# A norm shared by three engines, with a reordered start of the first mixer, in a four-block transformer kernel

## What is computed

```python
def rms_norm_2(x, g):
    xf = x.astype(jnp.float32)
    y = xf * lax.rsqrt(jnp.mean(xf * xf, axis=-1, keepdims=True) + NORM_EPS)
    return (y * g.astype(jnp.float32)).astype(x.dtype)

def ada_modulation(c, w, b):
    mod = jax.nn.silu(c) @ w + b
    shift, scale, gate = jnp.split(mod, 3, axis=-1)
...
        shift, scale, gate = ada_modulation(c, mw, mb)
        h = rms_norm_2(x, g) * (1.0 + scale) + shift
        x = x + gate * mixer(h, *mixer_params[layer])
```

## Time and profile before

| | us |
|---|---|
| median of three runs | 2342.48 |
| lowest, highest | 2342.39, 2344.87 |
| the profiled execution | 2344.19 |
| its span | 2342.4 |
| busy: TensorE, VectorE, GpSimd, ScalarE | 1880.9, 1307.9, 735.1, 607.1 |

### The profile page before, as it was taken

How to read it: one execution, slowest core, us unless ns; L and a number is a source line. 1 busy time by engine, 2 the same in 40 slices (tenths; PEclk the granted TensorE clock), 3 DMA queues, 4 the chain that set the end, 5 groups by cost and what they waited for, 6 DMA issues and landing times. The chain is left out here.

```text
span 2342.4 us, 20225 instructions
## 1 busy us (share of the span) xinstructions
PE 1880.9 (80%) x6462; PEld 998.1 (43%) x6462; DVE 1307.9 (56%) x3171; ACT 607.1 (26%) x1370; POOL 735.1 (31%) x695
## 2 busy tenths in 40 slices
PE   6987898959877898776868777988798886877877
PEld 4555332329645444332323336756444432323332
DVE  4454300027276656667676646545756667676663
ACT  3442111114622212221221214543222222222221
POOL 0000154410103343443544420330344344444441
PEclk9998899979988999998989897998899998998989
DMA  8843899958448999999999966543999999999995
GB/s 296 316 178 145 321 401 400 401 191 242 180 160 301 409 410 410 421 422 421 421 422 415 422 289 237 187 151 107 342 409 410 412 421 422 421 421 420 410 419 239
DMA packets 211846, 786.03 MB, mean 336 GB/s; under 512 B 29243, under 2 KB 89403, under 8 KB 145948
## 3 DMA queue, kind: packets, MB, share of 16 engines
q0 software_dynamic: 85408, 547.20, 56.9%
q1 hardware_dynamic: 126332, 237.53, 28.0%
HBM read 806.56 MB, written 13.98 MB: 350 GB/s over the span
## 5 line engine op out<-in xcount | busy, mean ns | idle before, releaser
L1802 PE MATMUL psum<-peer_rows,peer_diag 128*128 128x512 f32 x2048 | 980.0, 638 | 276.1 <-ACT peer_diag L1854 275.9
L1970 DVE CUSTOM_DVE_ANT_0 peer_rows<-peer_rows,peer_norm_h 128x1024 f32<-128x1024 f32 x512 | 620.1, 1225 | 445.2 <-DMA peer_rows<-in_peer_uv,peer_expert 444.9
L1891 POOL DMA_INDIRECT peer_rows<-in_peer_uv,peer_expert x512 | 582.6, 1138 | 880.9 <-PE psum L1802 667.4
L1802 PEld LDWEIGHTS psum<-peer_rows,peer_diag 128*128 128x128 f32 x2048 | 412.0, 205 | 828.2 <-issue 500.7
L1854 ACT ACTIVATE peer_diag<-ident,peer_weight 128x128 f32<-128x128 f32 x512 | 163.5, 390 | 727.6 <-DVE peer_weight L1980 727.6
L1197 PE MATMUL psum<-moe_ring,moe_W 128*64 128x512 f32 x640 | 145.4, 600 | 17.7 <-issue 12.7
L1781 PE MATMUL psum<-peer_norm_hT,peer_q_raw 128*128 128x256 f32 x512 | 123.7, 400 | 11.3 <-DMA peer_q_raw<-in_peer_q 8.1
L1781 PEld LDWEIGHTS psum<-peer_norm_hT,peer_q_raw 128*128 128x128 f32 x512 | 101.9, 201 | 37.1 <-DMA peer_q_raw<-in_peer_q 13.1
L1270 POOL COPY moe_W<-moe_X 128x512 f32 x40 | 24.3, 614 | 269.2 <-DVE moe_piece_i L1409 206.8
L1197 PEld LDWEIGHTS psum<-moe_ring,moe_W 128*64 128x64 f32 x640 | 46.7, 138 | 113.2 <-issue 113.0
L1848 ACT ACTIVATE peer_dots<-peer_dots 128x4 f32<-128x4 f32 x128 | 26.3, 206 | 262.6 <-DVE peer_dots L1970 259.4
(11 more groups left out here) (414 smaller groups left out, 2237.0 us busy)
## 6 DMA issues: line engine op xcount, KB each, us to landing
moe_ring<-in_moe_w SPq DMA_DIRECT2D x192, 512.0 KB, 10.1
mix_mod_w<-in_mod_w SPq DMA_DIRECT2D x32, 768.0 KB, 7.5
peer_q_raw<-in_peer_q SPq DMA_DIRECT2D x32, 512.0 KB
fox_w_raw<-in_fox_in SPq DMA_DIRECT2D x32, 512.0 KB
mix_w_raw<-in_w_in SPq DMA_DIRECT2D x24, 512.0 KB
lru_mod_w<-in_mod_w SPq DMA_DIRECT2D x16, 768.0 KB
fox_mod_w<-in_mod_w SPq DMA_DIRECT2D x16, 768.0 KB, 6.2
lru_in_raw<-in_lru_in SPq DMA_DIRECT2D x22, 512.0 KB, 4.7
```

The costliest lines, as they stand in the source:

```text
L1802: ins = pe.matmul(Y(t, c), diag[:, j % 2, k, :], R[:, place_of(m), D + c * BANK:D + (c + 1) * BANK], start=first and k == 0, stop=final an ...
L1891: pool.indirect_dma_start(R[:, place_of(m), :], None, uv, bass.IndirectOffsetOnAxis(ap=expert[:, t, at:at + 1], axis=0))\
L1970: dve.tensor_tensor_reduce(here, here, norm.h[:, t, :], 1.0, 0.0, ALU.mult, ALU.add, dots[:, t, at:at + 1]).then_inc(dotted, 1)
```

## The change

Four things change. (1) In the non-plain norms VectorE scales tiles 0 and 2 and ScalarE tiles 1 and 3, each into its own part of `h`, which has been turned by then; GpSimd rounds all four; VectorE subtracts. The buffers `v` stay allocated for the mixer's squares. (2) The first weights' rounding stands behind ScalarE's tile 1 and their subtraction behind VectorE's second low half: one piece in mix1 and lru, four in fox. (3) In mix1 SP loads the c column second and modulation pieces 0 to 3 among weight pieces 0 to 7; ScalarE computes the SiLU between the squares and the root, and reloads the root's table; TensorE takes modulation pieces 0 and 1 before the first weight piece, and piece n behind weight piece n. (4) In mix1 VectorE subtracts weight piece 1 before it copies the bias curve. The norms of moe and the peers keep their work.

```diff
-    def act(self, act):
+    def v_of(self, n):
+
+        t, g = n % 2, n // 2
+        return self.h[:, t, g * BANK:(g + 1) * BANK].rearrange("p (k n) -> p k n", k=4)
+
+    def affine(self, act, n, out):
+        act.wait_ge(self.turned, n + 1)
+        for k in range(4):
+            f, src = 4 * (n // 2) + k, self.bank(n % 2, n // 2)[:, k, :]
+            if self.mod is None:
+                ins = act.activation(out[:, k, :], src, ACT.Copy, scale=self.cols[:, f:f + 1])
+            else:
+                ins = act.activation(out[:, k, :], src, ACT.Identity, bias=self.cols[:, KD + f:KD + f + 1], scale=self.cols[:, f:f + 1])
+        return ins
+
+    def act(self, act, meanwhile=None, weights=None):
...
-        for n in range(2 * NT):
-            act.wait_ge(self.v_ready, n + 1)
-            act.copy(self.core.hTh[self.at(n % 2, n // 2)], self.v[:, n % 2]).then_inc(self.hT_act, 1)
+        for n in range(1, 2 * NT, 2):
+            self.affine(act, n, self.v_of(n)).then_inc(self.v_act, 1)
+            if n == 1:
+                weights()
+
+    def pool(self, pool):
+
+        for n in range(2 * NT):
+            pool.wait_ge((self.v_dve, self.v_act)[n % 2], n // 2 + 1)
+            pool.tensor_copy(self.core.hTh[self.at(n % 2, n // 2)], self.v_of(n)).then_inc(self.hT_pool, 1)
+            pool.wait_ge(self.hT_pool, n + 1)
...
-        for n in range(2 * NT):
-            t, g = n % 2, n // 2
+        for n in range(0, 2 * NT, 2):
             dve.wait_ge(self.turned, n + 1)
-            if n >= 2:
-                low(n - 2)
-                dve.wait_ge(self.hT_dve, n - 1)
...
+        for n in range(2 * NT):
+            at = self.at(n % 2, n // 2)
+            dve.wait_ge(self.hT_pool, n + 1)
+            dve.tensor_tensor(self.core.hTl[at], self.v_of(n), self.core.hTh[at].bitcast(F32), ALU.subtract).then_inc(self.hT_dve, 1)
+            if n == NT - 1:
+                weights()
...
                 norm.load(sp)
+                mods.load_c(sp)
                 sp.dma_start(table[0:N_BUCKETS, :], d["rel_bias"]).then_inc(table_landed, 16)
                 sp.dma_start(buckets[:, :], d["c_buckets"]).then_inc(table_landed, 16)
-                m.load(sp, 0, 8)
-                mods.load_c(sp)
+                m.load(sp, 0, 4)
+                mods.load(sp, 0)
+                mods.load(sp, 1)
+                m.load(sp, 4, 8)
+                mods.load(sp, 2)
+                mods.load(sp, 3)
...
                     m.load(sp, 8 + q, 9 + q)
-                    mods.load(sp, q)
+                    mods.load(sp, 4 + q)
...
                 norm.pe(pe)
+                for q in range(2):
+                    mods.pe(pe, q)
                 norm.hT_half(pe)
                 for n in range(12):
                     m.piece(pe, n)
                     if n >= 2:
-                        mods.pe(pe, n - 2)
-                for q in range(10, 12):
-                    mods.pe(pe, q)
+                        mods.pe(pe, n)
...
-                norm.act(act)
+                def silu():
+                    mods.act(act)
+                    core.root_table(act)
+
+                norm.act(act, meanwhile=silu, weights=lambda: m.round_to(act, 1))
                 m.round_to(act, 4)
-                mods.act(act)
...
-                norm.dve(dve)
+                norm.dve(dve, weights=lambda: m.subtract_to(dve, 1))
+                m.subtract_to(dve, 2)
                 dve.wait_ge(curve_done, 1)
```

More of the change, by code:

```diff
@@ L162, in at @@
         return slice(None), slice(4 * g, 4 * g + 4), slice(t * P, (t + 1) * P)
-    def act(self, act):
+    def v_of(self, n):
[11 more added lines that the diff above has]
+    def act(self, act, meanwhile=None, weights=None):
         act.activation(self.h[:, 0, :], self.core.x[:, 0, :], ACT.Square, accum_out=self.stat[:, 0, 0:1]).then_inc(self.squares_summed, 1)
+        if meanwhile is not None:
+            meanwhile()
         act.wait_ge(self.var_ready, 1)
@@ L254, in hT_half @@
     def hT_half(self, pe):
-        pe.wait_ge(self.hT_act, NT)
+        pe.wait_ge(self.hT_pool, NT)
         pe.wait_ge(self.hT_dve, NT)
     def hT_done(self, eng):
-        eng.wait_ge(self.hT_act, NT if self.plain else 2 * NT)
-        eng.wait_ge(self.hT_dve, NT if self.plain else 2 * NT)
+        if self.plain:
+            eng.wait_ge(self.hT_act, NT)
+            eng.wait_ge(self.hT_dve, NT)
+        else:
+            eng.wait_ge(self.hT_pool, 2 * NT)
+            eng.wait_ge(self.hT_dve, 2 * NT)
 class Stream:
@@ L758, in _ @@
                     m.load(sp, 8 + q, 9 + q)
-                    mods.load(sp, q)
+                    mods.load(sp, 4 + q)
                     if q == 4:
                         mods.load_bias(sp)
-                for q in range(12, 16 + mods.slots):
+                for q in range(16, 16 + mods.slots):
                     mods.load(sp, q)
@@ L778, in _ @@
                 pool.wait_ge(mods.b_clear, 2)
+                norm.pool(pool)
                 pool.wait_ge(curve_copied, 1)
@@ L1490, in _ @@
                     pool.wait_ge(padded, 1)
+                    norm.pool(pool)
                 @block.scalar
                 def _(act):
-                    norm.act(act)
-                    win.run(act, win.stream.round, 1)
+                    norm.act(act, weights=lambda: win.stream.round(act, 0, 0))
+                    win.run(act, lambda eng, base, b: win.stream.round(eng, base, b) if b else None, 1)
                 @block.vector
                 def _(dve):
-                    norm.dve(dve)
+                    norm.dve(dve, weights=lambda: win.stream.subtract(dve, 0, 0))
                     chain = Chain(dve, conv_chain)
@@ L1520, in work @@
                             dve.wait_ge(vec_landed, 16)
[L1521 removed]
+                        if b:
+                            win.stream.subtract(eng, base, b)
                         if LAG <= b < LAG + LBLK:
@@ L2142, in sigmoid @@
                         act.activation(og, og, ACT.Sigmoid).then_inc(og_ready, 1)
-                norm.act(act)
-                m.round_to(act, 4)
+                norm.act(act, weights=lambda: m.round_to(act, 4))
                 mod3.act(act)
@@ L2205, in gated @@
                         dve.tensor_tensor(v, v, m.proj[:, t, ogcol + half * BANK:ogcol + (half + 1) * BANK], ALU.mult).then_inc(m.y_ready, 1)
-                norm.dve(dve)
+                norm.dve(dve, weights=lambda: m.subtract_to(dve, 4))
                 chain = Chain(dve, chain_sem)
-                m.subtract_to(dve, 4)
                 chain.step(dve.memset(onerow[:, :], 1.0))
```

31 lines of the change are left out of this document (7 added, 24 removed).

## The result

The changed kernel takes **2340.15 us** (median of 20 runs, 2335.71 to 2344.21), the kernel before 2344.28 us on the same chips (median of 20, 2341.11 to 2350.78). The ratio is 0.9981 with a 95% interval of 0.9974 to 0.9988: 4.5 us faster by the ratio (2.8 to 6.1), 4.1 between the medians. The forecast of 2331.7 us was too low, and the range with it. The sign was right; more than half of the gain is missing.

A forecast was written before the change was run, and what follows sets the result against it. It took mix1 as bound by bytes up to its first scores, and lru and fox as held at their norm's head; gains of 4.8, 3.3 and 2.7 us sum to 10.8, forecasting 2331.7 us, range 2326 to 2338.

The forecast's parts named there:

- fill the hole: mix1, 19.7 to 26 us: modulation pieces 0 to 3, asked for earlier, use the stretch at 35 GB/s; 5.3 us gained.
- Rival 2: mix1: the hole only moves, or its gain goes into slow clock, c's load and SiLU; gain 0.5, 2336.0 us, chance 0.17.
- the cold clock: mix1, TensorE at its slow level after a wait, possibly before the scores: 0.9 us charged (0 to 2.7).
- lru: Head of lru: first weight matmul 3.9 us earlier through the norm's new path, less 0.6 for contention; 3.3 us gained.
- the clash: New norm: GpSimd's rounding of tile 2 meets VectorE's first low half; 0.6 us charged, between 0 and 1.3.
- fox: Head of fox: same new norm path, TensorE starts at 1420.1 instead of 1422.82; 2.7 us gained (1.8 to 3.3).
- GpSimd's price: New norm: GpSimd rounds a 128x512 tile into the high-half type in 0.61 us, like its copy; upper bound 2.0.
- rival 3: Norms of lru and fox: GpSimd's rounding is a slow path, losing 6 and 5 us; 2350 us, chance 0.06.

The follow-up runs named there:

- e2: The changed kernel with the old norm, keeping mix1's new order of loads and products; 2344.69 us, ratio 1.0011 to the kernel before.
- e3: The changed kernel with mix1's thirteen small loads issued on SP only after modulation piece 7, their users moved later; 2340.75 us, ratio 0.9984.
- e7: The changed kernel without mix1's thirteen small loads, computing with constants written by GpSimd instead; 2334.87 us, ratio 0.9964.
- e5: The changed kernel with ScalarE instead of GpSimd rounding all four tiles of the norm; 2337.07 us, ratio 0.9982.
- e9: The changed kernel with all thirteen small loads issued from GpSimd's queue behind the skewed store, their users moved later; 2340.64 us, ratio 0.9988.
- e1: The changed kernel with mix1's old order of loads and products, so the new norm alone; 2338.26 us, ratio 0.9986 to the kernel before.
- e6: The changed kernel with mix1's small loads issued by GpSimd, five behind its norm, eight behind the curve's store; 2337.88 us, ratio 0.9975.

## Why the prediction was wrong

**Wrong: "fill the hole".** The step that failed is the sentence that pieces 0 to 3 "fill the hole" of 35 GB/s, worth 5.3 us. I read a window with a share of 0.20 as missing requests. The rows of that stretch's packets would have told: 1428 of 2060 under 512 bytes, with thirteen small loads issued on SP between two groups of bulk loads. With them on SP's queue the transfers fall to some tens of GB/s in whatever order the bulk is asked for, and the bulk asked for behind them comes only when they are through (asked for at 27.28 us, moving at 33). The four modulation pieces put 3.1 MB ahead of the small loads, some 7.5 us at 417 GB/s, and the hole starts that much later, between 27 and 28 us instead of at 19.7, as long as it was. SP also became slower at issuing (4.02 us for two pieces), so the small loads and weight piece 8 were asked for 5 us later. e2 shows the moved hole with the old norm, e3 a third place, e7 its end. Rival 2 had this ("the hole only moves") at 0.17, and against it stood "the hole is plain"; plain it was, but I had not asked what was in it. Even rival 2 left mix1 0.5 us of gain, and mix1 lost 2.3 to 3.6.

**Mis-sized: the cold clock.** I charged 0.9 us (0 to 2.7) ahead of the scores. The cost came behind them. The seven profiles with a clock of 1.00 there have 121.3 to 122.8 us left, mean 121.8; the seven with 0.58 to 0.72 have 123.3 to 126.1, mean 124.0: 2.2 us. Why the new order starves TensorE more is my reading, which no run tests by itself: it takes two modulation pieces earlier and waits for the same bytes, so its waits fall just ahead of the scores (2.06 and 1.18 us at 86.22 and 89.33, against 1.70 at 81.71 and 0.79 at 89.22). Together mix1: the 5.3 is gone, the tail loses 2.2, and the scores are 0.6 later (92.1 against 91.5, means of two each): 2.8 us of loss. Between mix1's two means it is 3.6, as in those four profiles the tails differ by 3.0. In lengths with the small loads on SP, the old order has a mean of 206.7 (three) and the new one 209.0 (four), 2.3 us apart.

**Right: lru.** Three profiles with the old norm have 178.0 us on the mean (178.25, 177.71, 178.12), eleven with the new 173.76 to 175.50, mean 174.8: 3.2 us, forecast 3.3. (The eleven include e5, whose norm differs.) Its start came at 7.12 us for 7.5. Of the clash, charged at 0.6, 0.34 us lies on the low halves ahead of the start; the 0.33 on tile 3's rounding fell beside TensorE's first product and held nothing.

**Mis-sized: fox.** 214.6 us on the mean of three (213.86 to 214.98) against 210.5 of eleven (207.65 to 213.27): 4.1 us, forecast 2.7 (1.8 to 3.3). 2.9 of it is the head (9.42 to 6.50 us). Most of the rest is clock, in two places. The first: TensorE's first 512-wide products after and before, in the timelines of fox:

```profile
1428.29 0.77 PE L320 MATMUL psum<-fox_w_h,fox_hTh 128*128 128x512 f32 x1
...
1430.99 0.43 PE L320 MATMUL psum<-fox_w_h,fox_hTh 128*128 128x512 f32 x1
```

```profile
1433.05 0.77 PE L306 MATMUL psum<-fox_w_h,fox_hTh 128*128 128x512 f32 x1
...
1437.89 0.50 PE L308 MATMUL psum<-fox_w_h,fox_hTl 128*128 128x512 f32 x1
```

After, the full rate comes 2.7 us behind the first wide product, before 4.8 us behind it: five slow products fewer, at 0.43 us a step instead of 0.23, are 1 us. That is this pair of profiles: the three with the old norm take 4.9 to 5.1 us to the full rate, the ten with the changed norm, all with the same head, 2.8 to 5.1, mean 3.8; that makes it 0.6 us on the mean. The second is larger. Before and after, at TensorE's wait for the next weights:

```profile
1472.09 0.64 PE L306 MATMUL psum<-fox_w_h,fox_hTh 128*128 128x512 f32 x1 [2.69 <-DVE fox_w_l L295]
```

```profile
1466.28 0.48 PE L320 MATMUL psum<-fox_w_h,fox_hTh 128*128 128x512 f32 x1 [2.69 <-DVE fox_w_l L309]
```

Behind the same wait of 2.69 us the kernel before runs eight products at 0.43 us a step, the kernel after none: 1.6 us. All three profiles with the old norm have this slow stretch, and so have six of the ten with the changed one; those six have fox at 211.6 us on the mean, 2.9 shorter than before, which is the head alone and near the forecast of 2.7. The four without it (both of the changed kernel, e7, e9) have 209.4. I hadn't counted the clock here, and what decides whether it falls is not known, so as far as the forecast goes this part of the gain is luck.

**Right: GpSimd's price**, 0.61 us; rival 3 is dead. The rule that puts GpSimd at half of VectorE's speed (the Trainium skill, GPSIMD Engine Reference, section 3) isn't borne out for this rounding: 0.61 us, beside 0.68 for VectorE's low half of the same size.

**The sum.** 3.2 won in lru, 4.1 in fox and 2.3 to 3.6 lost in mix1 give 3.7 to 5.0 us, against the measured 4.5 (2.8 to 6.1). By the medians alone the split would not stand: e1 and e2 together give 3.3 won and 2.6 lost, 0.7 in all, with some 3 us of doubt on each, and the 7.3 us of lru and fox lie above e1's interval (0.7 to 6.1). It stands on the stage lengths and the rows.

**Open.** By the packets both sorts of small loads make the hole, some 3 us each: the rows first, then the gains. Whether fewer and larger descriptors for the same bytes on SP's queue would end it wasn't tried; e6's gains, in larger packets on another queue, change both at once. Nor is it known why mix1's first scores spread by 2.5 us in an unchanged kernel, nor why e5 escaped the cold start.

## What to carry to other kernels

A stretch of low GB/s is a hole to be filled only if its packets say that nothing was asked for: look at their count and size, and at what was issued just before, because a dozen small loads between bulk ones on one queue cost 5 us here and took the hole with them wherever they stood on it. Putting bulk ahead of them delays them and all that stands behind them on that queue. Where an engine is bound by bytes, giving it its products earlier makes it wait later, and a wait just ahead of dense work costs clock in that work as well.

## What the runs showed of the hardware that I had not expected

- Thirteen loads with 0.2 MB in all hold the transfers at 53 GB/s for 6 us (kernel after, 28 to 34 us), with the transfer engines busy 0.22 of the time; the loads of 4-byte packets alone leave 4 GB/s (kernel before, 23 to 26 us). The same eight gain loads from GpSimd's queue pass at 402 GB/s (e6, 34 to 40 us). The Trainium skill, DMA: Bandwidth & Descriptors, section Rules for kernel authors, says to coalesce small transfers, as under 64 KB one pays mostly overhead. The runs agree, and show that the bill goes to the bulk loads behind them on the same queue.
- SP's issue of a load, 0.38 to 0.6 us when the queue is short, takes 2 us when much is outstanding (two pieces in 4.02 us at 13.44, with ten pieces asked for since 8.10): the issuing queue itself becomes late.
- GpSimd's rounding to the high-half type costs the same as its copy, 0.61 us for 128x512, and when it meets VectorE's subtraction both stretch, 0.61 to 0.94 and 1.36 to 1.70 for a pair.
- Behind the same wait of 2.69 us in fox TensorE's granted clock was at its lower level in nine of thirteen profiles (e5 left out) and at the full one in four, and the four have fox 2.2 us shorter than the six others of the same norm.
